# A hybrid diffusion step on one core: the even layer's two attentions in one loop, its projection tail, its output in two halves, and the order at the head and in the odd layer

## The chip, the cores and the metric

The kernel runs on one NeuronCore of a Trainium2 chip. TensorE (PE) multiplies, VectorE (DVE) and ScalarE (ACT) work on vectors and read PSUM, GpSimd (POOL) does elementwise work in SBUF, SyncE (SP) issues the transfers. The metric is the device time of one execution in microseconds, the median of the runs.

## The reference

One inference step of a trunk of two layers for 128 context tokens and 512 latent tokens (640 in all), with a model width of 1024. Each layer is a half-step SwiGLU FFN (hidden width 2816), a mixer, and another half-step FFN, each with an RMSNorm whose scale, shift and gate come from a conditioning vector. The final RMSNorm gives the outputs.

The mixer of the even layer is what the change is mostly about:

```python
cq, ckv, krope, qd, kd, vd = jnp.split(h @ w_in, EVEN_CUTS, axis=-1)
q = (rmsnorm(cq, q_norm) @ w_uq).reshape(b, t, H_A, NOPE_A + ROPE_A)      # 8 heads of 64 + 32
kv = (ckv @ w_ukv).reshape(b, tk, H_A, NOPE_A + V_A)
o_a = mla_attend(q_nope, q_rope, kv[..., :NOPE_A], krope, kv[..., NOPE_A:])
o_b = diff_attend(q1, q2, k1, k2, vd, lam)          # softmax(s1) - lam * softmax(s2), 4 heads of 2 x 64
o_b = rmsnorm(o_b, subln) * (1.0 - lam_init)
return jnp.concatenate([o_a, o_b], axis=-1) @ w_out
```

Latent tokens get a rotary turn of q and k and read 128 cached tokens and all 640 of their step less the context's own (640 keys); context tokens read only the 128 context tokens and get no rotary turn. The odd layer's mixer has two bidirectional gated recurrences, worked in chunks of 128 tokens. Outputs beside the two token arrays are the new caches and states of the context tokens.

## The kernel before

**Layout and arithmetic.** Activations lie with features on partitions: `x` is 8 tiles of 128 features x 640 tokens. A product of the projections and FFNs is exact to fp32 through three products of split numbers: `hh`/`hl` are the high and low part of the normed input, `wh`/`wl` those of a weight unit, and `part_products` does high x high, high x low and low x high, each in two pieces of the token axis (384 and 256, with two more columns that carry the shift of the norm, so 386). Lines 2502, 2504 and 2506 of the profile are these three. A weight unit (1 MB) is loaded by SP to `raw`, copied to `wh` by ACT (`split`, line 2157), and `wl = raw - wh` is made by POOL (`split_lo`, line 2117). There are two slots. `unit_tile` is 8 contraction tiles x 3 products x 2 pieces.

**The norm.** `norm_sum` (lines 2537, 2538) sums the squares over partitions on PE, ACT makes `rstd` (lines 2162 to 2164, Ln then Exp), and the tiles of the next product are scaled by `rstd` only when DVE takes them out of PSUM (`scaled_out`, line 335). So the product can start before `rstd` is known, but PSUM is freed only after. ACT's `z_high` (line 2177) and DVE's `z_low` (line 2346) make `hh` and `hl`.

**Order.** Each engine has one queue, written out by hand, and counts on semaphores hold them together. The phases are ffn0, even, ffn1, ffn2, odd, ffn3.

**The head.** x is turned on PE; `mshift` and then `mscale` (4 MB each) are loaded; PE multiplies them with `cs` (line 2629, 16 matmuls of 2 x 512 for each); ACT copies the two rows out (line 2263), PE turns them to columns, DVE adds the bias (line 2471), then `z_consts`, `z_high` and `z_low`, and the first tile of ffn0.

**The even layer.** `even_pe` runs nine units (7 in `EVEN_T`, two value units in `EVEN_TOK`), two tiles each, and after the first unit it does `norm_sum` and waits for `rstd`. With units 5 to 8 it multiplies the q and k tiles by a rotation matrix (`rotate`, line 875), and DVE forms the rotary turn in three operations (`roped`, lines 711 to 713). After the last unit come: turning five value tiles (line 861), the rotation of the shared rotary key, turning the caches and the context's outputs, the queries head by head (8 products of 96 rows, each with its own rotation of 96 x 512), values of the latent attention (lines 954 to 956), and the keys of head 0 (lines 972 to 974).

Then 40 steps of latent attention (8 heads x 5 blocks of 128 queries), and only then 20 steps of differential attention. For one step: scores on PE into one of two PSUM buffers (`scores_a`, lines 987 to 990; `scores_d`, lines 1045 to 1048, two score arrays for one step), the row maximum on DVE (line 789), the exponential on ACT (line 629), the scaling on DVE (line 819; for a differential step 839, 840 and 842), the transposes of the probabilities on PE (`turn_p`, line 861), their copies on ACT (636, 637), the product with the values on PE (`weigh`, line 1018) and its copy by DVE (804, 806). After each differential head comes `diff_norm` (lines 678 to 684 on ACT, 1056 and 1057 on PE, 811 on DVE); for heads 0 to 2 PE waits in its queue for ACT's result. The last head's norm stands ahead of the output product. `out_pe` takes four units of 256 output columns with all 8 contraction tiles.

**The odd layer.** Its output product already runs in two halves of four contraction tiles (`out_tile`), among the last steps of the recurrence. POOL makes the low parts of the first half (line 1213) in its queue between two weight units. DVE forms `qret` (line 1684) between the second and the third state update.

Of the kernel before, what the change touches and what calls it, by code (L numbers as in the profile page):

```python
# [66 lines left out]
EVEN_T = (0, 256, 512, 672, 928, 1184, 1440)  # L67
EVEN_TOK = (1696, 1952)
# [5 lines left out]
EVEN_UNITS = len(EVEN_T) + len(EVEN_TOK) + 3 + OUT_UNITS  # L74
# [45 lines left out]
def build(nc, a, phases=PHASES):  # L120
# [79 lines left out]
    mrow, _ = view("mrow", [2, 2 * D], at_a + 4 * (TOK // P + DT) * D, end_a)  # L200
# [12 lines left out]
    head_in = [sem("shift_in"), sem("scale_in")]  # L213
    head_mm, mrow_ok = sem("head_mm"), sem("mrow_ok")
# [46 lines left out]
    for name in phases:  # L261
# [5 lines left out]
        else:  # L267

            res_base[name] = n_res
            n_res += 8 if name == "odd" else 4  # L270
# [29 lines left out]

    proj_mm = [sem("proj_mm0"), sem("proj_mm1")]
# [6 lines left out]
    proj_n = {"even": (0, 0, 0), "odd": ((len(EVEN_T) + len(EVEN_TOK), 5, DT) if "even" in phases else (0, 0, 0))}  # L308
# [4 lines left out]

    def turned_unit_pe(pe, unit_tile, n0, done, r):

        pe.wait_ge(w_lo, n0 + 1)
        for m in range(2):
            pe.wait_ge(res_ok[m], res_before[phases[r]])
            if done:
                pe.wait_ge(scaled[m], done)  # L320
            unit_tile(n0 % 2, m, DT, wide(hh), wide(hl), wide_of((psG, psU)[m], 0), True, True,
                      (lambda k: input_split(pe, r, k)) if m == 0 else None).then_inc(proj_mm[m], 1)
# [22 lines left out]
    def turned_values(pe, turn, src, first, done):  # L345

        for j in range(TOK // P):
            if done + j >= 2:
                pe.wait_ge(v_turned[(done + j) % 2], (done + j) // 2)
            ps = (psG, psU)[(done + j) % 2][:, 2, :]  # L350
            for k in range(4):
                ins = turn(ps[:, k * P:(k + 1) * P], src[:, first + k, j * P:(j + 1) * P])
            ins.then_inc(v_turn, 1)

    def values_out(eng, copy, side, dst, done):

        for j in range(TOK // P):
            if (done + j) % 2 == side:
                eng.wait_ge(v_turn, done + j + 1)
                copy(dst(j), (psG, psU)[side][:, 2, :]).then_inc(v_turned[side], 1)  # L360

# [18 lines left out]
    def out_act(act, split, res_squares, z_high, z_shift_high, name, base):  # L380
        r = norm_of[name] + 1
        last = name == phases[-1]

        def pair(i, s, more):
            o = i * 2 + s
            z_high(r, o, 0, res_base[name] + 1)
            if more:
# [2348 lines left out]
```

## Time and profile before

| | before |
|---|---|
| median of 3 runs | 2878.29 us (2877.61 to 2880.95) |
| the profiled execution's own time | 2879.18 us |
| its span | 2877.9 us |
| PE busy | 2739.2 us, 95% of the span |
| DVE, ACT, POOL busy | 1614.4, 921.8, 1030.1 us |
| mean granted TensorE clock | 0.974 |
| HBM traffic | 89 GB/s over the span |

The span is the time from the first to the last instruction. Engines overlap, so their busy times do not add up. A granted clock of 1.0 is 2.4 GHz, 0.5 is 1.2 GHz, and what stands between them is a mean over a stretch with both. Matmuls are pipelined, so the busy time of PE counts a matmul at half the clock as twice as long.

### The profile page before, as it was taken

The page shows a single profiled execution, that of the slowest core. Times are in us where ns is not written, and L with a number is a line of the kernel's source. Part 1 is how long each engine was busy: PE and PEld are TensorE (multiplying, and loading weights), DVE is VectorE, ACT ScalarE, POOL GpSimd, SP SyncE. Part 2 cuts the span into 40 slices and gives each one's busy share as a digit, 9 for nine tenths or more (in the row PEclk, how much of TensorE's full clock was granted, in tenths as well). Part 3 has the DMA queues.
Part 4 walks back from the last instruction along what each step waited for, and adds up shares of the span by engine and source line. Part 5 has one row for each costly group of instructions (what it writes and reads, how often), then busy time and mean ns, then how long its engine had stood idle before and what let it go on. Part 6 is the DMA issues. An engine that isn't in the chain of part 4 may idle for free.

```text
span 2877.9 us, 45113 instructions
## 1 busy us (share of the span) xinstructions
PE 2739.2 (95%) x17963; PEld 2612.1 (91%) x17963; DVE 1614.4 (56%) x2410; ACT 921.8 (32%) x1236; POOL 1030.1 (36%) x300
## 2 busy tenths in 40 slices
PE   6999999998798799999999999999999899999997
PEld 3999999997576599999999999999998799999997
DVE  4888598426556558943885898214474653111124
ACT  3322122442245543321224331123432544321222
POOL 1434344433101024443444344435431313444442
PEclk9999999999898799999999999999999999999999
DMA  6443442321100023423423443221321112222211
GB/s 245 132 142 114 137 147 79 110 74 45 40 1 16 1 73 122 141 81 124 146 90 130 146 132 117 74 81 55 107 59 52 57 40 73 73 66 81 72 60 64
DMA packets 210124, 258.90 MB, mean 90 GB/s; under 512 B 4964, under 2 KB 170472, under 8 KB 210024
## 3 DMA queue, kind: packets, MB, share of 16 engines
q1 hardware_dynamic: 209352, 254.88, 26.9%
q10 hardware_dynamic: 672, 2.62, 0.2%
q8 instruction: 71, 1.16, 0.2%
q14 instruction: 29, 0.24, 0.0%
HBM read 253.66 MB, written 3.82 MB: 89 GB/s over the span
## 4 chain that ended last, share of the span: by engine, by line
PE 86%; DVE 5%; issue 5%; POOL 2%; ACT 2%; DMA 1%; SPq 0%; DVEq 0%; ACTq 0%; POOLq 0%
PE psU L2506 12%; PE psU L2502 12%; PE psU L2504 12%; PE psG L2502 12%; PE psG L2506 12%; PE psG L2504 12%; PE psB L1018 2%; POOL wl L2117 2%; PE psG L861 1%; ACT pr L629 1%; PE psG L987 1%; PE psU L987 1%; DMA mshift<-in_mod_w 1%; PE psG L1045 1%; PE psG L2629 0%
## 5 line engine op out<-in xcount | busy, mean ns | idle before, releaser
L2117 POOL TENSOR_TENSOR wl<-raw,wh 128x2048 fp32r<-128x2048 f32 x185 | 867.7, 4691 | 1219.9 <-ACT wh L2157 1219.9
L2157 ACT CAST wh<-raw 128x2048 fp32r<-128x2048 f32 x185 | 353.3, 1910 | 717.4 <-PE psU L2506 440.9
L2301 DVE SCALAR_TENSOR_TENSOR macc<-mraw,cs,macc 128x512 f32<-128x512 f32 x448 | 488.0, 1157 | 0.0
L2502 PE MATMUL psG<-hh,wh 128*128 128x386 f32 x1744 | 407.7, 315 | 21.2 <-DVE hl L2346 16.8
L2502 PE MATMUL psU<-hh,wh 128*128 128x386 f32 x1760 | 404.2, 311 | 1.5 <-issue 1.5
L2506 PE MATMUL psU<-hh,wl 128*128 128x386 f32 x1760 | 404.7, 311 | 0.0
L2504 PE MATMUL psU<-hl,wh 128*128 128x386 f32 x1760 | 404.1, 311 | 0.0
L2506 PE MATMUL psG<-hh,wl 128*128 128x386 f32 x1744 | 402.8, 312 | 0.0
L2504 PE MATMUL psG<-hl,wh 128*128 128x386 f32 x1744 | 401.9, 312 | 0.0
L2128 POOL TENSOR_TENSOR al<-af,ah 128x640 f32 x88 | 131.6, 1496 | 467.8 <-ACT ah L2214 467.8
L2502 PEld LDWEIGHTS psG<-hh,wh 128*128 128x128 f32 x1744 | 271.4, 191 | 25.8 <-POOL wl L2117 11.1
L2502 PEld LDWEIGHTS psU<-hh,wh 128*128 128x128 f32 x1760 | 271.3, 190 | 3.0 <-issue 2.7
L2504 PEld LDWEIGHTS psU<-hl,wh 128*128 128x128 f32 x1760 | 270.9, 189 | 0.0
L2504 PEld LDWEIGHTS psG<-hl,wh 128*128 128x128 f32 x1744 | 270.2, 190 | 0.0
L2506 PEld LDWEIGHTS psU<-hh,wl 128*128 128x128 f32 x1760 | 270.2, 189 | 0.0
L2506 PEld LDWEIGHTS psG<-hh,wl 128*128 128x128 f32 x1744 | 269.1, 190 | 0.0
L2214 ACT CAST ah<-af 128x640 f32 (+1 forms) x88 | 63.8, 725 | 531.3 <-DVE af L2425 531.3
L2418 DVE TENSOR_TENSOR af<-psU,rstd 128x386 f32<-128x386 f32 (+1 forms) x176 | 74.3, 485 | 268.8 <-PE psU L2506 268.8
L2410 DVE TENSOR_TENSOR sg<-psG,rstd 128x386 f32<-128x386 f32 (+1 forms) x176 | 74.1, 483 | 194.6 <-PE psG L2506 194.6
L2361 DVE SCALAR_TENSOR_TENSOR x<-psG,hgate,x 128x384 f32 (+1 forms) x132 | 49.9, 434 | 230.9 <-PE psG L2506 230.9
L2502 PE MATMUL psG<-ah,wh 128*128 128x384 f32 x704 | 162.3, 312 | 10.1 <-POOL wl L2117 10.1
L2504 PE MATMUL psG<-al,wh 128*128 128x384 f32 x704 | 160.9, 310 | 0.0
(552 smaller groups left out, 4056.4 us busy)
## 6 DMA issues: line engine op xcount, KB each, us to landing
mraw<-in_mod_w SPq DMA_DIRECT2D x64, 1024.0 KB, 5.0
raw<-in_ffn_w_gate SPq DMA_DIRECT2D x44, 1024.0 KB, 5.3
raw<-in_ffn_w_up SPq DMA_DIRECT2D x44, 1024.0 KB, 5.2
raw<-in_ffn_w_down SPq DMA_DIRECT2D x32, 768.0 KB, 4.3
raw<-in_ffn_w_down SPq DMA_DIRECT2D x32, 640.0 KB, 4.0
raw<-in_odd_w_in SPq DMA_DIRECT2D x12, 1024.0 KB, 5.2
raw<-in_even_w_in SPq DMA_DIRECT2D x9, 1024.0 KB, 5.1
mshift<-in_mod_w SPq DMA_DIRECT2D x1, 4096.0 KB, 14.6
```

What stands on the lines that cost most here:

```text
L987: nc.tensor.matmul(buffers(s)[:, 0:512], q, kt[:, h % 2, 0:512], start=True, stop=True)
L1018: ins = nc.tensor.matmul(out, v, pt[:, n % 2, k], start=k == 0, stop=k == kn - 1)
L2117: nc.gpsimd.tensor_tensor(wl[:, slot], raw[:, slot], wh[:, slot].bitcast(F32), ALU.subtract).then_inc(w_lo, 1)
L2128: nc.gpsimd.tensor_tensor(tile_of(al, i * 2 + m), af[:, m, SH:WID], tile_of(ah, i * 2 + m).bitcast(F32), ALU.subtract).then_inc(a_lo, 1)
L2157: nc.scalar.copy(wh[:, slot], raw[:, slot]).then_inc(w_hi, 1)
L2214: nc.scalar.copy(tile_of(ah, i * 2 + m), af[:, m, SH:WID]).then_inc(a_hi, 1)
L2301: ins = nc.vector.scalar_tensor_tensor(out=macc[:, c], in0=mraw[:, s, k], scalar=scalar, in1=macc[:, c], op0=ALU.mult, op1=ALU.add)
L2410: ins = nc.vector.tensor_tensor(sg[:, m, a0:a1], ps, rstd[:, a0:a1], ALU.mult)
L2418: ins = nc.vector.tensor_tensor(af[:, m, a0:a1], ps, rstd[:, a0:a1], ALU.mult)
L2502: nc.tensor.matmul(ps, lhs_h, rhs_h[:, lo:hi], start=first, stop=False)
L2504: nc.tensor.matmul(ps, lhs_h, rhs_l[:, lo:hi], start=False, stop=False)
L2506: ins = nc.tensor.matmul(ps, lhs_l, rhs_h[:, lo:hi], start=False, stop=last)
```

## The change

1. The projection of the even layer has its units in another order: the two value units come fourth and fifth. The turns of the values, the rotation of the shared key and six of the eight head rotations stand between projection tiles. `norm_sum` stands after the first tile, and PE no longer waits for `rstd` there.
2. The queries are six products of 128 rows in place of eight of 96: for four heads two products of the position-free parts (two heads each) and one of the four rotary parts. `query_parts` reorders the columns when ACT and POOL split the weights, so that two rotations of 128 x 512 serve all heads. The splits of both query units stand in the projection. ACT takes over the copies of the turned caches and outputs.
3. The attention steps run in one sequence `SEQ`: one differential step, two latent steps, 18 times, then four latent and two differential steps. Score arrays are counted in units, and `AHEAD` says how far their matmuls run ahead.
4. The differential norm is done once for all heads after the last step, in five matmuls of 512 columns.
5. The output product runs in two halves of four contraction tiles, the first with the latent heads. Two of its tiles stand in the last steps of the attention. Each output tile gets its residual addition twice.
6. At the head the scale is loaded and worked first, the shift after the first weight unit. Each of the two products is four column groups of 256 output columns (partitions 0, 32, 64, 96), and ACT and DVE share the copies. `z_high` and `z_low` run before the shift is there.
7. In the odd layer DVE makes the low parts in place of POOL, and `qret` stands after the last state update.

The core of the diff:

```diff
+EVEN_PROJ = ((0, 0), (256, 2), (512, 4), (1696, 14), (1952, 16), (672, 6), (928, 8), (1184, 10), (1440, 12))
...
+    HEAD_BANKS = (psA, psB, psG[:, 2, :], psU[:, 2, :])
+    def head_rows(eng, copy, side, b):
+        eng.wait_ge(head_mm, b + 1)
+        for g in (side, side + 2):
+            ins = copy(mrow[32 * g:32 * g + 2, b], (psG, psU)[b][32 * g:32 * g + 2, 0, 0:2 * P])
+        ins.then_inc(mrow_ok[side], 1)
...
+    SEQ = []
+    for _i in range(18):
+        SEQ += [D_STEPS[_i], A_STEPS[2 * _i], A_STEPS[2 * _i + 1]]
+    SEQ += A_STEPS[36:] + D_STEPS[18:]
...
+    AHEAD = [min(UNIT_OF[n + 1] + 2, N_SCORES) for n in range(NS)]
...
+        # PE
+        def head_rotated(c):
+            u = 5 + c // 2
+            pe.wait_ge(proj_ok[c % 2], u + 1)
+            rotate(1 + c, 1, P, proj[:, ROPED[c], 0:T_LAT])
+        def queries(i):
+            n = EB + EU + i // 3
+            pe.wait_ge(w_lo, n + 1)
+            ps = (psG, psU)[i % 2]
+            for k in range(3):
+                pe.wait_ge(e_lo, k + 1)
+                w = slice(k * 384 + i % 3 * P, k * 384 + (i % 3 + 1) * P)
+                ins = part_products(wh[:, n % 2, w], wl[:, n % 2, w], cqh[:, k], cql[:, k], runs_alone(ps), k == 0, k == 2)
+            ins.then_inc(e_q, 1)
+        tile(0, 0)
+        norm_sum(r, mods_at["even"])
+        tile(0, 1)
...
+        tile(5, 0)
+        for m in range(2):
+            pe.wait_ge(proj_ok[m], 5)
+        values(0)
+        values(1)
+        tile(5, 1)
+        pe.wait_ge(e_rt, 2)
+        rotate(0, 0, ROPE_A, proj[0:ROPE_A, KR, 0:T_LAT])
+        values(2)
+        values(3)
+        tile(6, 0)
+        values(4)
...
+        for n in range(NS):
+            if next_keys(n) is not None:
+                head_keys(next_keys(n), n)
+            for u in range(AHEAD[n - 1] if n else UNIT_OF[1], AHEAD[n]):
+                scores(u)
+            if n == NS - 1:
+                weigh(n - 1)
+                pe.wait_ge(e_ex, N_SCORES)
+                out_tile(0, 0)
+                turn_p(n)
+            else:
+                turn_p(n)
+                if n:
+                    weigh(n - 1)
+        out_tile(0, 1)
+        weigh(NS - 1)
+        out_tile(0, 2)
+        out_tile(0, 3)
+        pe.wait_ge(d_sq, 4)
+        pe.wait_ge(e_o, NS)
+        means(psA[:, :], n_sqd[:, :, T_LAT:TOK])
...
+        # DVE, one step of the loop
+            for v in range(u, UNIT_OF[n + 1]):
+                inverse(v)
+            if kind == "A":
+                nc.vector.tensor_scalar(p1, p1, stat[:, 3, u % 4:u % 4 + 1], None, ALU.mult).then_inc(e_p, 1)
+            else:
...
+            if n >= 2:
+                heads_out(n - 2)
+            if next_keys(n) is not None:
+                keys_out(next_keys(n))
+            for v in range(AHEAD[n - 1] if n else UNIT_OF[1], AHEAD[n]):
+                maximum(v)
...
     def odd_pool(pool, st, split_lo):
-        for k in range(H_C):
-            pool.wait_ge(o_hi, o0 + k + 1)
-            nc.gpsimd.tensor_tensor(odd_l(k), feat[:, GR + k], odd_h(k).bitcast(F32), ALU.subtract).then_inc(o_lo, 1)
...
+        # odd layer, DVE, ahead of scaled(11, 0)
+        for k in range(H_C):
+            dve.wait_ge(o_hi, o0 + k + 1)
+            nc.vector.tensor_tensor(odd_l(k), feat[:, GR + k], odd_h(k).bitcast(F32), ALU.subtract).then_inc(o_lo, 1)
...
-        for b, w in enumerate((mshift, mscale)):
+        for b, w in enumerate((mscale, mshift)):
             pe.wait_ge(head_in[b], 16)
-            for half in range(2):
-                for k in range(DT):
-                    ins = nc.tensor.matmul((psG, psU)[b][0:2, half, :], cs[:, k], w[:, k, half * 512:(half + 1) * 512],
+            for k in range(DT):
+                for g in range(4):
+                    ins = nc.tensor.matmul((psG, psU)[b][32 * g:32 * g + 2, 0, 0:2 * P], cs[:, k], w[:, k, g * 2 * P:(g + 1) * 2 * P],
                                            start=k == 0, stop=k == DT - 1)
```

## Rows read from the trace of the kernel before

**Rows 1.** Stretches: us; PE, PEld, DVE, ACT, POOL busy; PE clock; DMA share; GB/s.
```profile
694.60:713.80 19.20, 8.84 (x38) 5.75 (x37) 15.13 (x21) 4.84 (x10) 8.20 (x3) 0.67 0.00 1
...
774.70:892.00 117.30, 116.12 (x708) 84.82 (x709) 70.41 (x202) 57.53 (x156) 0.00 (x0) 1.00 0.00 1
892.00:1017.40 125.40, 95.16 (x436) 67.88 (x434) 75.14 (x209) 64.31 (x146) 15.15 (x7) 0.74 0.03 9
```

**Rows 2.** Timeline of the head: start, us, engine, line, operation, idle before.
```profile
20.40 13.89 PE L2629 MATMUL psG<-mshift,cs 128*2 128x512 f32 x32 [2.73 <-DMA mshift<-in_mod_w]
...
34.13 13.90 PE L2629 MATMUL psU<-mscale,cs 128*2 128x512 f32 x32
...
55.41 11.80 DVE L2346 SCALAR_TENSOR_TENSOR hl<-x,g,hh 128x512 fp32r<-128x512 f32 x16
...
60.83 0.87 PE L2502 MATMUL psG<-hh,wh 128*128 128x386 f32 x2 [11.06 <-DVE hl L2346]
```

**Rows 3.** DMA issues: transfer, count, KB, us from issue to landing.
```profile
mshift<-in_mod_w SPq DMA_DIRECT2D x1, 4096.0 KB, 14.6
mscale<-in_mod_w SPq DMA_DIRECT2D x1, 4096.0 KB, 24.3
```

**Rows 4.** Timeline of PE, products into column halves, odd layer.
```profile
2273.94 1.04 PE L1793 MATMUL psB<-rv,kst_r 128*64 128x128 f32 x16
```

**Rows 5.** The chain that ended last, at the norm of the even layer.
```profile
563.46 0.65 PE psA L2537 x2
...
568.93 0.87 PE psG L2502 x2
...
574.62 0.45 PE psG L2504 x2
```

**Rows 6.** Timeline of PE: projection, then the tail up to the first scores.
```profile
692.86 1.02 PE L875 MATMUL psA<-proj,rot 128*128 128x512 f32 x2
...
703.26 1.11 PE L861 MATMUL psU<-ident,vt_e 128*128 128x128 f32 x4 [5.29 <-DVE vd L360]
...
735.53 0.82 PE L2502 MATMUL psU<-cqh,wh 128*96 128x384 f32 x2 [6.25 <-issue]
...
774.71 1.10 PE L987 MATMUL psG<-kt,qa 96*128 96x512 f32 x2 [0.73 <-DVE kt L781]
```

**Rows 7.** Timeline of DVE and POOL, same tail.
```profile
695.43 4.88 DVE L713 TENSOR_TENSOR proj<-proj,rope_e 128x512 f32<-128x512 f32 x1
...
701.79 0.69 DVE L713 TENSOR_TENSOR proj<-proj,rope_e 128x512 f32<-128x512 f32 x1
...
695.03 4.72 POOL L2117 TENSOR_TENSOR wl<-raw,wh 128x2048 fp32r<-128x2048 f32 x1 [11.13 <-ACT wh L2157]
```

**Rows 8.** Timeline of the attention, all engines.
```profile
802.57 1.13 PE L987 MATMUL psG<-kt,qa 96*128 96x512 f32 x2
...
804.40 1.31 PE L1018 MATMUL psB<-pt,va 128*64 128x128 f32 x10
805.63 1.13 PE L987 MATMUL psU<-kt,qa 96*128 96x512 f32 x2
...
931.14 0.89 DVE L842 SCALAR_TENSOR_TENSOR pr<-pr,stat,pr 128x640 f32<-128x640 f32 x1
...
932.14 0.81 DVE L789 TENSOR_REDUCE stat<-psG 128x1 f32<-128x640 f32 x1
...
933.24 0.79 ACT L629 ACTIVATE pr<-psG,stat 128x640 f32<-128x640 f32 x1 [2.41 <-DVE stat L790]
```

**Rows 9.** Waits of PE between 893 and 1018 us: total, times, longest.
```profile
PE psB L1018 <- ACT af L684: 9.3, 3, 3.1
PE psG L861 <- DVE pr L842: 8.7, 8, 1.7
```

**Rows 10.** Timeline of PE at the ends of the odd layer's output.
```profile
2298.29 0.79 PE L1830 MATMUL psU<-am,rv 128*128 128x128 f32 x2 [7.75 <-DVE am L1533]
...
2387.87 0.57 PE L2502 MATMUL psG<-hh,wh 128*128 128x386 f32 x2 [1.89 <-DVE hl L2346]
```

More of the change, by code:

```diff
@@ new lines, in even_act @@
+        log_of(3, n_sqd[:, 1, 0:T_LAT], bank_g)
+        log_of(4, n_sqd[:, 2, 0:T_LAT], bank_u)
+        log_of(5, n_sqd[:, 3, 0:T_LAT], psA[:, :])
+        act.wait_ge(d_ln, 5)
+        for h in range(H_B):
+            nc.scalar.activation(n_sqd[:, h], n_sqd[:, h], ACT.Exp, scale=-0.5).then_inc(d_rt, 1)
+        act.wait_ge(down_mm[1], rb + 2)
+        split(EB + EU + 5)
+        for k in range(4, 8):
+            act.wait_ge(o_ok, o0 + k + 1)
+            copy(even_h(k), proj[:, QD + k - 4]).then_inc(o_hi, 1)
@@ L686, in even_dve @@
+        act.wait_ge(down_mm[1], rb + 4)
+        split(EB + EU + 6)
+        act.wait_ge(stored, 16 * 4)
+        z_shift_high(r)
+        more = phases[-1] != "even"
+        for o in range(4):
+            z_high(r, o, 0, rb + 5)
+            if more and o % 2:
+                act.wait_ge(down_mm[1], rb + 4 + o + 1)
+                split(EB + EU + 7 + o // 2)
+            z_high(r, o, 1, rb + 5)
+            for m in range(2):
+                res_squares(r, o, m, rb + 5)
     def even_dve(dve, st, residual, add_squares, gate_of, z_low, z_consts):
@@ new lines, in even_pe @@
+        values(3)
+        tile(6, 0)
+        values(4)
+        tile(6, 1)
+        head_rotated(0)
+        head_rotated(1)
+        tile(7, 0)
+        tile(7, 1)
+        head_rotated(2)
+        head_rotated(3)
+        tile(8, 0)
+        head_rotated(4)
+        head_rotated(5)
+        tile(8, 1)
+        pe.wait_ge(scaled[0], EU)
+        queries(0)
+        pe.wait_ge(scaled[1], EU)
+        queries(1)
+        head_rotated(6)
+        head_rotated(7)
+        for side in range(2):
+            pe.wait_ge(e_qo[side], 1)
@@ new lines, in means @@
+        def means(bank, src):
+            nc.tensor.matmul(bank, ones[:], src, start=True, stop=True).then_inc(d_mm, 1)
+        pe.wait_ge(c_out, 4)
+        for side in range(2):
+            pe.wait_ge(e_qo[side], 4)
+        pe.wait_ge(e_qr, 2)
+        pe.wait_ge(e_roped, 9)
+        for u in range(UNIT_OF[1]):
+            scores(u)
+        pe.wait_ge(e_roped, 11)
+        pe.wait_ge(e_qc, 2)
+        pe.wait_ge(e_kr, 1)
+        head_keys(0, 0)
+        for side in range(2):
+            pe.wait_ge(e_vo[side], 3)
@@ L1074, in build @@
+        for t in range(8):
+            out_tile(1, t)
     OB = unit_base.get("odd", 0)
```

978 lines of the change are left out of this document (493 added, 485 removed).

## The prediction

> **What bounds the kernel now.** The page first: TensorE is busy for 2739.2 of 2877.9 us. The four FFN phases are filled, so a gain can only come from stretches in which PE stands still, runs at half clock, or does work that goes away. The table of stretches shows three kinds in the even layer [rows 1]. Between 694.6 and 713.8 us PE is busy for 8.8 of 19.2 us at a mean clock of 0.67. The latent attention (774.7 to 892.0) keeps PE at 116.1 of 117.3 us with the clock at 1.00: PE is its bound. The differential attention (892.0 to 1017.4) has PE at 95.2 of 125.4 us with the clock at 0.74, while DVE has 75.1 and ACT 64.3: no engine is full, and a chain from engine to engine sets the pace. The timeline of the head shows PE's two products of 13.9 us each and the first tile of ffn0 at 60.83 [rows 2]. The chain that ended last has a hole at the even layer's norm [rows 5].
>
> **The head.** PE's start of ffn0 is the end of one chain: shift loaded at 20.3, two products, rows out, `hh`, `hl`. In the new order the scale is the first 4 MB and lands at 20.3 as the shift did [rows 3]. Its product has the same 8192 output columns, in four groups of partitions. Lower bound of the time: four at once, 13.9 / 4 = 3.5 us; upper bound: one after the other, 13.9. The nearest rows: eight products of 128 columns that alternate between two column halves (16 records) take 1.04 us, 0.13 each [rows 4]; five of the same width in one half (10 records) take 1.31, 0.26 each [rows 8]. Two halves do run at once; I take four, 3.5 us, so 24. ACT splits the first weight unit first, then rows, turns and bias take the 4.6 us that lie between the last product (48.0) and `hh` now, so `hh` begins near 28.5. `hl` takes 11.8 us for 16 operations with one POOL split over it [rows 2], so 40.5. The shift comes third in the queue: the second 4 MB landed at 6.2 + 24.3 = 30.5 [rows 3], and one unit of 1 MB lies between, so 33.5; 3.5 of product, then the same 4.6 us, slowed by ACT's second split: 43 to 44. PE starts 16 us earlier (8 if the groups run in turn: 34.3 + 13.9 + 4 = 52).
>
> A page of the Trainium skill weighs against the four at once: "TensorE: Matmul & The Clock Gate", Part 3, gives three column tiles a measured 2.38 times, not 3. By it, as an estimate, the product takes 13.9 / 3.2 = 4.4 us and the head gives 15. No row here has four groups.
>
> **The norm.** PE waits from 564.5 to 568.93 and runs at half clock until 575.07: 4.4 us and half of 5.7, so 7 us [rows 5]. After the change the sum comes one tile (7.1 us) earlier, and the second tile hides the 3 us of ACT. What is late next is DVE's reading of the first tile, 4 us before PE wants that bank. Gain 7.
>
> **Moved into the projection.** Five value tiles of four turns (1.11 us at half clock, so 0.55 at full) and one rotation (two take 1.02 us and more, records overlapping; 0.86 each between their starts) [rows 6] stand in PE's queue between tiles: +3.7 with their gaps, all on the path. DVE's and ACT's copies lie beside tiles of 7.1 us.
>
> **The tail up to the first scores.** Now 692.86 to 774.71, 81.9 us [rows 6]. Its holes: 5.3 us at the values, 6.3 at the second query unit's split, others before rotations, each with a stretch at half clock behind it. What is left after the change, at full clock: six query products of 3 x 3 x 0.295 = 2.65 us (15.9; eight now), two head and two query rotations (3.4; ten now), 14 turns of caches and outputs (3.0), 36 value products of 0.23 (8.3): 31 us. I add 3 for the handshakes between query products and ACT's or DVE's copies: 34. Gain 48. What hides the splits: both query units are split while PE works tiles 8 and 9, the unit for the values while PE does three query products and 14 turns (13 us against 1.9 + 4.7). If the cover goes, the queue of DVE is the cause: it has 8.4 us of query rotation behind a POOL split. Bounds of the gain: 38 (one lock of 4.7 us at each of two places) and 51.
>
> **The attention loop.** PE's work: the latent part stays at 116. A full latent step takes 805.63 - 802.57 = 3.06 us [rows 8]. A differential step is one score array more, 1.07: 4.13; 16 of these and four short ones of 1.0 make 70. Together 186 us against 242.7 now. Can ACT and DVE follow? For one group of a differential and two latent steps (18 of them) PE has 4.13 + 2 x 3.06 + 0.8 (share of the keys) = 11.0 us. DVE: four maxima of 0.93, two latent scalings with copies (0.95), the differential scaling (two reciprocals, 0.55, 0.19, 0.89 and a copy: 2.4), keys 0.5: 8.5 us. ACT: four exponentials of 0.9, three pairs of copies of 0.75, 0.5: 6.4 us. So PE remains the largest. In order of time: the exponentials of the differential step end at 0; its scaling ends at 1.9; the next two maxima end at 3.1 and 4.1; ACT's next exponential ends at 4.05, when PE ends the turns and products it has (3.9) and takes the next score array; the group closes at 10.2. It is nearly without slack on DVE, so I charge 1 us of wait to each group, 18 us, from nothing (the latent part loses 1.2 us in 117 now) up to 2 us a group. First latency +3, two output tiles that now lie in the last steps +7, last step +1: 215. Gain 28 (10 to 44). The norm waits of 9.3 us and the 8.7 us for the scaling [rows 9] are within what goes. PE's clock, 0.74 now, must be near 1.00 for this.
>
> **The output.** Before: 1017.4 to the norm sum of ffn1 at 1085.8, 68.4 us. After: 14 of 16 tiles of 3.55 (49.7), five means of 0.86 (4.3), the first FFN tile 7.1, and waits: 1.5 for the first residuals, 1.5 for ACT's split and POOL behind the norm, 3 at the end, as the odd layer's same form has 1.89 for the last `hl` [rows 10]. That is 67: gain 1 (-4 to +3). The second addition to x costs DVE 8 x 1.1 us beside PE.
>
> **The odd layer.** PE waits 7.75 us for DVE [rows 10]. DVE loses some 4 us less to POOL's low parts and takes 3.3 us for four of its own; `qret` only changes its place ahead of the same reading of tile 11. Gain 2 (-1 to 5).
>
> **Sum.** 16 + 7 - 3.7 + 48 + 28 + 1 + 2 = 98 us. The profiled execution took 2879.2, so 2781; the median of the runs shown is 0.9 lower: 2780.
>
> **Rivals.** (a) DVE becomes the bound of the loop. It has 8.5 of 11.0 us, and it serves in order: a maximum stands behind a scaling that waits for ACT (ACT's 2.41 us of idle before an exponential is that wait [rows 8]). At 13 us a group: +36, 2816. Against it: the hand schedule closes at 10.2. (b) POOL holds DVE. An addition of two SBUF tiles took 4.88 us beside a split of 4.72, and 0.69 without [rows 7]. In the loop lie two splits and four low parts of about 1.6 us, 16 us of POOL, and in the tail two splits. If all of it lands on the path: +16 to +20, 2799. The Trainium skill states it as a lock ("SBUF — State Buffer", Who interferes with whom): the later of the two blocks wholly, and copies in some modes too. The trace agrees for two inputs. (c) The column groups run in turn: +8, 2788. (d) The other side: the loop does not overlap. Each step then waits for its own chain (scores 1.08, maximum 0.97, exponential 0.9, scaling 0.7, turns 0.75, copy 0.75, product 1.23: 6.4 us, 7.9 for a differential one), 20.7 us a group, +170 us: 2950. It decides from 16.5 us a group on. For it: the differential part does take 6.3 us a step. Against it: the latent part, with the same two buffers, takes 3.06.
>
> **Chances.** The forecast (2765 to 2792) 0.55; (a) 0.14; (b) 0.12; (c) 0.06, inside the likeliest range's edge; better than forecast (loop or tail at the upper ends) 0.07; (d) or another large new wait 0.06, two thirds of it slower than before. The range is 2762 to 2812. Faster by over 0.2% (5.8 us, what a measurement here can tell from no change): 0.94; within: 0.02; slower: 0.04.
>
> **What would show it.** PE's first tile of ffn0 near 44 us, and the first product (scale) ending near 24. No wait for `rstd` behind the first even tile. From the last projection tile to the first scores 34 us. In the loop, PE over 90% busy, clock 1.00, 11 to 12 us for a group, and about 215 us from the first scores to the last value product. Wrong if PE's waits for DVE's scaling in the loop exceed 30 us, if the clock stays under 0.9 there, or if the tail exceeds 45 us.

## The result, and the profile after

The changed kernel took 2808.53 us (median of 4 executions, 2803.39 to 2813.54), the kernel before 2877.95 beside it: ratio 0.9755, interval 0.9739 to 0.9771. Forecast were 2780 and a range of 2762 to 2812. So 69 us were gained where 98 were forecast: the direction and the range hold, the point does not, and the sum behind it is wrong in two places, the attention loop above all.

The profiled execution took 2813.54 us against 2879.18, 65.6 less. Cut at the same events of PE in both traces (its first tile of ffn0; the first even tile behind the wait for `hl`; the end of the last projection tile, which for the kernel before is the rotation at 692.86; the first scores; the end of the last value product; the norm sums of the next phases), the two stand so. For the kernel before, the attention is counted to 1017.4, as in the prediction: that is the sum of the last differential norm, 1.15 us behind the end of its last value product at 1016.25. "Again" is a second trace of the changed kernel, from an execution of 2806.17 us.

| stretch | before | after | again | forecast gain | gain in the profiled pair |
|---|---|---|---|---|---|
| head, up to PE's first tile of ffn0 | 60.83 | 45.58 | 45.16 | 16 | 15.3 |
| ffn0, to the first even tile | 494.4 | 497.7 | 497.1 | 0 | -3.3 |
| projection, with the norm and what moved in | 137.7 | 134.3 | 134.4 | 7 - 3.7 | 3.3 |
| tail, to the first scores | 81.9 | 34.4 | 31.8 | 48 | 47.4 |
| attention, first scores to last value product | 242.7 | 233.5 | 233.4 | 28 | 9.2 |
| output, to the norm sum of ffn1 | 68.4 | 74.7 | 70.7 | 1 | -6.3 |
| ffn1 and ffn2 | 967.8 | 968.0 | 966.4 | 0 | -0.2 |
| odd layer | 336.0 | 334.6 | 336.5 | 2 | 1.3 |
| ffn3, to the end of the span | 488.4 | 489.3 | 489.5 | 0 | -1.0 |

The views of the profile after, in the order of the steps. First the head, a timeline (start, us, engine, line, operation, idle before and what ended it), which answers to [rows 2]:

```profile
21.23 5.21 PE L2768 MATMUL psG<-mscale,cs 128*2 128x256 f32 x64 [3.72 <-DMA mscale<-in_mod_w]
...
27.13 4.50 POOL L2232 TENSOR_TENSOR wl<-raw,wh 128x2048 fp32r<-128x2048 f32 x1 [25.15 <-ACT wh L2272]
28.50 3.16 DVE L2604 SCALAR_TENSOR_TENSOR g<-mod,vec 128x16 f32<-128x16 f32 x1
...
34.64 5.33 PE L2768 MATMUL psU<-mshift,cs 128*2 128x256 f32 x64 [6.61 <-DMA mshift<-in_mod_w]
...
40.91 4.50 POOL L2232 TENSOR_TENSOR wl<-raw,wh 128x2048 fp32r<-128x2048 f32 x1 [9.28 <-ACT wh L2272]
...
42.78 2.66 DVE L2613 TENSOR_TENSOR hl<-mod,hh 128x16 fp32r<-128x16 f32 x1 [0.40 <-ACT hh L2303]
```

The product of 13.9 us takes 5.21 in four column groups. But the mean clock was 0.69 in these 5.21 us and 1.00 in the 13.89 of the kernel before. Three later traces of the same product ("order taken back", "paired, other order around" and "head wait") have the clock at 1.00 there, and it takes 3.63 us; this is "head wait":

```profile
21.09 3.63 PE L2769 MATMUL psG<-mscale,cs 128*2 128x256 f32 x64 [2.31 <-DMA mscale<-in_mod_w]
```

Two DVE operations of 16 columns last 3.16 and 2.66 us (the second takes 0.18 in "head wait"): each ends when POOL's operation beside it does (27.13 + 4.50, 40.91 + 4.50).

Then three stretches of the even layer (us; PE, PEld, DVE, ACT, POOL busy; PE clock; DMA share; GB/s): the tail, the attention, the output. The second answers to the last two of [rows 1].

```profile
677.60:712.00 34.40, 31.35 (x168) 26.45 (x166) 17.21 (x30) 19.16 (x41) 14.99 (x6) 0.95 0.32 103
712.00:945.50 233.50, 215.74 (x1189) 155.22 (x1188) 148.64 (x412) 104.58 (x284) 10.69 (x5) 0.95 0.02 7
945.50:1020.20 74.70, 65.08 (x396) 61.26 (x395) 52.80 (x86) 33.64 (x46) 19.20 (x4) 0.95 0.22 75
```

The tail's 47.4 us can be read from such lines. Before, PE stood for 26.1 of 81.9 us at a mean clock of 0.79; now it stands for 3.1 of 34.4 at 0.95. So 23 us are holes that are gone, 15.5 are time at the lower clock (0.21 x 81.9 less 0.05 x 34.4), and 9 are work that went away or moved. No run takes the tail's parts back one by one, so what each of them is worth was not shown.

In the attention PE is at 92% busy and its clock at 0.95 instead of 0.87 over the two parts. Yet it is only 9 us shorter. This is what PE works at a differential step there, from the timeline:

```profile
743.60 1.12 PE L1102 MATMUL psG<-proj 64*128 64x512 f32 x2
744.56 0.38 PE L1102 MATMUL psG<-kdc,proj 64*128 64x128 f32 x2
744.87 0.33 PE L928 MATMUL psG<-ident,pr 128*128 128x128 f32 x1
745.04 1.28 PE L1129 MATMUL psB<-pt,vd 128*128 128x128 f32 x10
746.25 1.12 PE L1102 MATMUL psU<-proj 64*128 64x512 f32 x2
747.21 0.38 PE L1102 MATMUL psU<-kdc,proj 64*128 64x128 f32 x2
```

Each of the two score arrays of a differential step takes 1.27 us (743.60 to 744.87, 746.25 to 747.52), with a value product between them. Last, PE's waits (who for whom: total, times, longest), first in the attention (714 to 945 us), then in the output (945.4 to 1020.2):

```profile
PE psG L1102 <- ACT pr L663: 6.3, 7, 1.2
...
PE psG L928 <- DVE pr L886: 4.4, 8, 1.4
...
PE psG L928 <- DVE pr L881: 3.6, 4, 2.7
```

```profile
PE psG L2641 <- DVE ml_b L908: 5.6, 2, 3.6
PE psG L2641 <- DVE hl L2462: 1.9, 1, 1.9
PE psG L2641 <- DVE x L2477: 1.6, 1, 1.6
```

### The profile page after: what moved, and what is told of

Same layout as the page of the kernel before. It is cut to its first block, busy times and chain, and to the rows that moved or that the text cites. A ratio compares the mean times of both kernels' runs of the same rounds, so it can differ in the third digit from the quotient of the medians.

```text
span 2812.2 us, 44951 instructions
## 1 busy us (share of the span) xinstructions
PE 2705.7 (96%) x17973; PEld 2597.5 (92%) x17973; DVE 1598.1 (57%) x2432; ACT 914.6 (33%) x1252; POOL 1010.4 (36%) x294
## 4 chain that ended last, share of the span: by engine, by line
PE 85%; DVE 6%; issue 4%; ACT 2%; POOL 2%; DMA 0%; SPq 0%; DVEq 0%; ACTq 0%; POOLq 0%
PE psU L2645 13%; PE psU L2641 13%; PE psU L2643 13%; PE psG L2641 12%; PE psG L2645 12%; PE psG L2643 12%; PE psB L1129 2%; POOL wl L2232 1%; PE psG L1102 1%; PE psU L1102 1%; PE psG L928 1%; DVE stat L853 1%; DVE rstd L2487 1%; ACT wh L2272 0%; PE psB L2636 0%
## 5 line engine op out<-in xcount | busy, mean ns | idle before, releaser
L2232 POOL TENSOR_TENSOR wl<-raw,wh 128x2048 fp32r<-128x2048 f32 x183 | 858.2, 4690 | 1077.7 <-ACT wh L2272 1077.7
L2477 DVE SCALAR_TENSOR_TENSOR x<-psG,hgate,x 128x384 f32 (+1 forms) x144 | 54.3, 432 | 241.2 <-PE psG L2645 241.2
L2641 PE MATMUL psG<-ah,wh 128*128 128x384 f32 x704 | 162.9, 313 | 10.2 <-POOL wl L2232 10.2
L2645 PE MATMUL psG<-ah,wl 128*128 128x384 f32 x704 | 161.5, 311 | 0.0
```

What stands on the lines that cost most here:

```text
L2232: nc.gpsimd.tensor_tensor(wl[:, slot], raw[:, slot], wh[:, slot].bitcast(F32), ALU.subtract).then_inc(w_lo, 1)
L2641: nc.tensor.matmul(ps, lhs_h, rhs_h[:, lo:hi], start=first, stop=False)
L2645: ins = nc.tensor.matmul(ps, lhs_l, rhs_h[:, lo:hi], start=False, stop=last)
```

## The experiments

All are edits of the changed kernel unless the text says otherwise. Ratios are to the kernel before, on the same chip; one kernel's executions scatter by up to 15 us here, so a difference of a few microseconds is read from the stretches and not from the total. Attention and output are these stretches in microseconds, each from one trace (233.5 and 74.7 in the first trace of the change, 242.7 and 68.4 before).

| kernel | median us | ratio, interval | attention | output |
|---|---|---|---|---|
| again | 2807.62 | 0.9753 (0.9739, 0.9766) | 233.4 | 70.7 |
| order taken back | 2806.13 | 0.9746 (0.9731, 0.9761) | 231.0 | 70.7 |
| scores paired | 2809.85 | 0.9754 (0.9741, 0.9768) | 234.2 | 74.6 |
| paired, other order around | 2814.97 | 0.9775 (0.9762, 0.9788) | 236.4 | 70.7 |
| before, without the four norms | 2854.43 | 0.9910 (0.9895, 0.9925) | 221.0 | - |
| short maximum | 2791.22 | 0.9685 (0.9671, 0.9700) | 216.4 | 70.8 |
| short maximum, paired | 2790.53 | 0.9684 (0.9669, 0.9699) | 219.6 | 74.8 |
| low parts on DVE | 2806.68 | 0.9740 (0.9727, 0.9753) | 230.3 | 74.8 |
| output split early | 2796.99 | 0.9714 (0.9701, 0.9728) | 231.6 | 66.9 |
| head wait | 2803.87 | 0.9739 (0.9725, 0.9752) | 228.5 | 74.6 |
| head wait and output split | 2800.00 | 0.9719 (0.9706, 0.9732) | 228.4 | 66.9 |
| all three small ones | 2802.71 | 0.9720 (0.9704, 0.9735) | 231.4 | 67.0 |

**Again.** The changed kernel, not edited.

> The changed kernel once more, unchanged. Its four executions lay between 2803.4 and 2813.5 us, so the same is expected: 2803 to 2814, with a second trace that tells which of the numbers of the first are steady. Theory 1 (the stretch of ffn0, 497.7 us from PE's first tile to the first even tile against 494.4 before, holds a steady new wait of 3.5 us for POOL's low part at 273): the wait and the 497.7 come again. Rival (it is a chance meeting of DVE and POOL): the stretch falls back to about 494.5, and the execution is near 2804 to 2806.

Theory 1 came out: in each further trace of the changed head PE waits 3.2 to 3.6 us for POOL's low part near 273 us, 2.1 before. So 1 to 3 us of the head are given back in ffn0. What makes that unit late was not traced further. The attention came out at 233.4 again; the tail and the output differ by 2.6 and 4.0 between two traces of one kernel, through waits and what the clock does behind them.

**Order taken back.**

```diff
-    for _i in range(18):
-        SEQ += [D_STEPS[_i], A_STEPS[2 * _i], A_STEPS[2 * _i + 1]]
-    SEQ += A_STEPS[36:] + D_STEPS[18:]
+    SEQ += D_STEPS[:18] + A_STEPS + D_STEPS[18:]
```

> The order of the steps alone is taken back: 18 differential steps, then all 40 latent ones, then the last two differential ones; all else is as in the change. Theory (the interleaving itself brought the gain of the loop): the differential part runs at its chain again, about 6.3 us a step and half clock for much of it, the latent part at 3.1 us a step; 18 x 6.0 + 40 x 2.95 + the last two steps and two output tiles (about 18) = 244 to 252 from the first scores to the last value product, against 233: kernel 2819 to 2827. Rival (the interleaving brought nothing, the gain came from elsewhere in the stretch): within 3 us of the change.

The rival came out: 231.0 us against 233.4 and 233.5. The edit does one thing more than its name says. Where differential steps follow each other, the look-ahead takes in both score arrays of a step, and PE works them side by side, or overlapped in part (766.48 and 767.35):

```profile
782.06 0.69 PE L1100 MATMUL psG<-proj 64*128 64x512 f32 x1
782.07 0.69 PE L1100 MATMUL psU<-proj 64*128 64x512 f32 x1
```

In the change they stand apart, and PE's busy time in the stretch is 215.7 us against 207.4 here. The kernel that interleaves and has them together is "scores paired" below, and it takes 234.2. So with either look-ahead, interleaving the two attentions, which names the change, gains nothing here. The stretches of this kernel, the 18 differential steps and then nearly all latent ones:

```profile
710.60:799.00 88.40, 71.02 (x372) 50.77 (x372) 66.77 (x186) 38.80 (x104) 0.00 (x0) 0.88 0.03 10
799.00:912.00 113.00, 111.76 (x681) 81.13 (x679) 69.07 (x191) 58.13 (x154) 8.10 (x4) 1.00 0.00 1
```

A differential step by itself takes 4.9 us (88.4 / 18), not the 6.3 (125.4 / 20) of the kernel before [rows 1]. Something else was in those 125.4 us.

**The kernel before, without the four norms of the differential heads.**

```diff
-            if i in (8, 13, 18):
-                diff_norm_act(act, st, (i - 8) // 5)
...
-            if i in (8, 13, 18):
-                diff_norm_sum((i - 8) // 5)
-                pe.wait_ge(d_rt, (i - 8) // 5 + 1)
...
-            nc.vector.scalar_tensor_tensor(out=proj[:, QD + h], in0=proj[:, QD + h], scalar=vec[:, g:g + 1], in1=af[:, 1, 0:TOK],
-                                           op0=ALU.mult, op1=ALU.mult).then_inc(o_ok, 1)
+            nc.vector.tensor_copy(lam[:, 3:4], lam[:, 1:2]).then_inc(o_ok, 1)
```

> The kernel before the change, with the norms of the four differential heads left out: no squares, sums, logarithms, exponentials and products for them, and no waits for them (the output is then not the reference's). Theory 2, formed from the order that was taken back: it was these norms, ten us of standing engines each, and not the chain of a differential step, that made the differential part long before. Without them a full step takes 4.8 us as in the order taken back: 16 x 4.8 + 4 x 3.1 = 89 instead of 125.4, so the two attentions take 206 to 212 instead of 242.7, and the kernel 2842 to 2850 (some further microseconds at the last norm). Rival, the reading of the prediction (each differential step is held by its own chain at 6.3 us, the norms add only their 9.3 us of waits): the loop stays at 231 to 235 and the kernel at 2866 to 2871.

221.0 us: 21.7 less than before (20.5 up to the same event, the end of the last value product), between the two expectations (12 above theory 2's middle, 12 below the rival's). From one head to the next, PE's value products lie 30.8 us apart in the kernel before (948.24 to 979.07) and 24.3 here (961.54 to 985.79). So a norm costs 6.6 us in the loop, more than twice the wait that it is booked with in [rows 9]. Theory 2 was wrong to count a short step at 3.1: the 24.3 us are 4.9 a step with the short one in it. The holes can be seen in the kernel before, two stretches of 10 us:

```profile
940.00:950.00 10.00, 5.10 (x21) 3.55 (x21) 3.63 (x14) 7.50 (x16) 0.00 (x0) 0.67 0.00 0
...
970.00:980.00 10.00, 4.84 (x20) 3.07 (x19) 3.48 (x14) 7.87 (x18) 0.00 (x0) 0.71 0.01 2
```

PE and DVE are at about half or less and ACT at 75% and more: square, logarithm and exponential stand in ACT's queue ahead of the exponentials of the next step. The timeline of the kernel before has this norm from its square to PE's next value product:

```profile
941.16 0.76 ACT L678 ACTIVATE af<-proj 128x640 f32<-128x640 f32 x1
941.93 1.28 ACT L682 ACT_TABLE_LOAD   x1
...
946.15 1.28 ACT L684 ACT_TABLE_LOAD   x1
947.45 0.74 ACT L684 ACTIVATE af<-af 128x640 f32<-128x640 f32 x1
...
948.24 2.50 PE L1018 MATMUL psB<-pt,vd 128*128 128x128 f32 x10 [3.09 <-ACT af L684]
```

ACT is in the norm for 7.0 us, and 2.6 of them are two loads of its function table, one ahead of the logarithm and one ahead of the exponential. The kernel before has eight such loads for its four norms, the change two (946.63 and 962.92).

The change takes the norms out of the loop and makes them in the output, all at once. The two output tiles of some 4 us that now lie in the stretch leave 221.0 + 8 = 229, and the changed kernels measured 228 to 234. So the norms that left are enough for the loop's whole gain.

**Scores paired.** The look-ahead of PE and DVE never ends between the two score arrays of a differential step.

```diff
     AHEAD = [min(UNIT_OF[n + 1] + 2, N_SCORES) for n in range(NS)]
+    AHEAD = [v - 1 if v - 1 in [UNIT_OF[d] for d in range(NS) if SEQ[d][0] == "D"] else v for v in AHEAD]
```

> The two score arrays of a differential step are issued next to each other again (the look-ahead never stops between them). Theory 1: side by side, in partitions 0 to 63 and 64 to 127, the two take about 1.3 us together (in the kernel before, 936.05 to 937.60 for both), apart 1.27 each; 16 full steps give PE 16 x 1.2 = 19 us less work in the loop (213 us busy now, about 195 then). The look-ahead loses one step, so part comes back as waits: by DVE's and ACT's chain (two maxima, two exponentials, the scaling of 2 us) a group closes at about 10.7 us instead of the 11.7 measured, so the loop goes from 233 to 215 to 225 and the kernel is 8 to 18 us faster than the change: 2790 to 2800. Rival A (the look-ahead is worth more than the pairing): PE's waits grow by more than 19 us, the loop stays at 233 or above, kernel 2805 to 2825. Rival B (they do not overlap even when adjacent): PE's busy time stays at 213 and nothing is won.

Its timeline at such a step, and its stretch:

```profile
779.08 0.81 PE L1103 MATMUL psG<-proj 64*128 64x512 f32 x1
779.10 0.81 PE L1103 MATMUL psU<-proj 64*128 64x512 f32 x1
779.73 0.59 PE L1103 MATMUL psG<-proj 64*128 64x512 f32 x1
779.74 0.59 PE L1103 MATMUL psU<-proj 64*128 64x512 f32 x1
```

```profile
712.40:946.50 234.10, 198.75 (x1189) 144.00 (x1188) 150.48 (x412) 105.30 (x284) 10.66 (x5) 0.96 0.02 6
```

The two arrays, 64 partitions each, do run at once: PE's busy time falls by 17.0 us (215.7 to 198.8). Its work without what the lower clock stretches is 189 us (198.8 less 0.04 x 234.1), less than the 194 that the prediction counted. Rival A came out all the same: the time comes back as waits, PE's for DVE's scaling go from 8.0 to 23.4 us:

```profile
PE psG L929 <- DVE pr L882: 17.1, 11, 2.7
PE psG L929 <- DVE pr L887: 6.3, 15, 1.4
```

**Paired, with another order around it.** The diff shows PE's and ACT's part; DVE takes `heads_out(n - 2)` ahead of its scaling.

```diff
+            elif n and "D" in (SEQ[n][0], SEQ[n - 1][0]):
+                weigh(n - 1)
+                turn_p(n)
...
+            if n >= 1 and SEQ[n - 1][0] == "D":
+                turned(n - 1)
             for u in range(UNIT_OF[n], UNIT_OF[n + 1]):
                 exponentials(u)
```

> The pairing of the differential scores together with another order around it: at a differential step and the one behind it PE takes the value product of the step before ahead of the turns, ACT copies the turned differential step out ahead of the next exponential, and DVE takes heads out ahead of the scaling. Theory 1 (with the scores paired PE has 198 us of work in 233, and stands for DVE's scaling, 23 us, because the value product that could fill that time is queued behind the turns): the waits for the scaling fall from 23 to 8 to 14 us, the loop from 234 to 219 to 226, the kernel 8 to 15 us under the paired one: 2795 to 2802. Rival (the chain of DVE and ACT of 11.7 us a group is full whatever PE does): the loop stays within 3 us of 234, the waits only change their names.

The rival came out, 236.4 us. The waits for the scaling fell as forecast (23.4 to 9.9 us), and new ones took their place: 8.4 us for ACT's copy of the turned step, 8.6 for DVE's copies out of psB.

**Short maximum, paired and unpaired.** A row maximum over a fifth of the columns gives the same softmax as long as nothing overflows, which nothing excludes for other inputs.

```diff
-            st.link(nc.vector.tensor_reduce(stat[:, 0, u % 4:u % 4 + 1], buffers(u)[:, 0:n_keys(j)], AX.X, ALU.max))
+            st.link(nc.vector.tensor_reduce(stat[:, 0, u % 4:u % 4 + 1], buffers(u)[:, 0:P], AX.X, ALU.max))
```

> The same short maximum in the kernel of the change, with its scores unpaired. Theory 3 (there PE's own work, 205 us without the two output tiles' 8, is the bound, and of DVE only the 17 us of waits and the half clock behind them are to be had): the loop 233 -> 217 to 225, so less than with the paired scores, and PE's clock 0.98 to 1.00 in it; kernel 2790 to 2800. Rival (DVE's chain is the bound here too): the loop gives as much as in the paired kernel, to 214 or below.

> The differential scores paired, and DVE takes the row maximum over the first 128 of the 640 columns only (0.29 us instead of 0.82; softmax is the same with any shift that does not overflow). Theory 3 (with the scores paired the loop is held by DVE's serial chain of maxima, exponentials and scaling, 11.8 us a group, and PE, 198 us busy of 233, waits): four maxima a group become 0.53 us shorter each, 2.1 us, two to four of them on the chain: 18 groups x 1.1 to 2.1 = 20 to 38 us, bounded by PE's own work of 186 to 198 us: the loop 234 -> 200 to 214, kernel 2775 to 2790. Rival (DVE is not what the chain waits for; ACT or the two score buffers set 11.8 us): the loop stays above 228, kernel above 2802.

The attention of the unpaired and of the paired kernel:

```profile
712.30:928.80 216.50, 207.77 (x1189) 149.96 (x1188) 116.40 (x412) 104.92 (x284) 10.69 (x5) 0.98 0.02 7
```

```profile
711.40:930.90 219.50, 197.03 (x1189) 145.50 (x1188) 117.22 (x412) 103.67 (x284) 10.67 (x5) 0.95 0.02 6
```

Both kernels gain 16 to 17 us in total (2791.2 and 2790.5), the best of the study. (Against "again"; the ratios say some 20.) With 32 us less on DVE the unpaired loop falls by 17, just past its expectation, and PE is busy for 96% at a clock of 0.98: here PE is the bound. In the paired one theory 3 is half right: 219.5, 5 above its range and well under the rival's 228, with 22.5 us of PE idle still. So DVE's maxima are on the chain in both; why the paired loop does not go below PE's new work stays open. It is not DVE's total, which is 117 of 219.5 us.

**Output split early.**

```diff
+        act.wait_ge(down_mm[1], rb + 2)
+        split(EB + EU + 5)
         log_of(5, n_sqd[:, 3, 0:T_LAT], psA[:, :])
...
-        act.wait_ge(down_mm[1], rb + 2)
-        split(EB + EU + 5)
         for k in range(4, 8):
```

> ACT splits the third weight unit of the output ahead of the fifth logarithm, in the 3.7 us in which it waits for the fifth mean, instead of behind the exponentials. Theory 1: POOL's low part (5.0 us) then lies at about 960 to 965, ahead of DVE's four norm products (7.6 us beside it, 4.5 without), so PE's 5.6 us of waits for the low parts of the mixed values and 2 to 4 us of half clock behind them go or shrink: stretch of the output 74.7 -> 67 to 70, kernel 5 to 8 us faster than the change. Rival (PE waits there for the chain of means, logarithms and exponentials, POOL's part is hidden anyway): the wait stays above 4 us, nothing is won or up to 2 us lost.

Theory 1 came out: the stretch takes 66.9 us, the clock is 1.00 in it, and PE's wait for `ml_b` is gone, 1.3 us more of waits for the residuals against it. DVE's four norm products and four low parts in the change and then in this kernel:

```profile
966.79 7.59 DVE L903 SCALAR_TENSOR_TENSOR proj<-proj,vec,n_sqd 128x640 f32<-128x640 f32 x4
...
968.72 4.98 POOL L2232 TENSOR_TENSOR wl<-raw,wh 128x2048 fp32r<-128x2048 f32 x1 [31.81 <-ACT wh L2272]
...
975.35 7.35 DVE L908 TENSOR_TENSOR ml_b<-proj,mh_b 128x640 fp32r<-128x640 f32 x4
```

```profile
961.89 3.26 DVE L903 SCALAR_TENSOR_TENSOR proj<-proj,vec,n_sqd 128x640 f32<-128x640 f32 x4
966.12 3.02 DVE L908 TENSOR_TENSOR ml_b<-proj,mh_b 128x640 fp32r<-128x640 f32 x4
```

The same instructions take 3.26 and 3.02 us without a POOL operation beside them. The total fell by 10.6 us against "again", more than the 4 to 8 of the stretch; the rest is scatter elsewhere in the traces.

**Head wait.** POOL waits for the shift's low part.

```diff
+        pool.wait_ge(sh_lo, 1)
         split_lo(1, 1)
```

> POOL makes the low part of the second weight unit of ffn0 only when the low part of the shift is there. Theory 1 (the small operation on the shift took 2.66 us instead of 0.2 because POOL's part of 4.5 us had begun at 40.91, and PE's first tile waited for it): PE starts ffn0 at 42.7 to 43.3 instead of 45.2 to 46.9, kernel 2 to 3 us faster: 2804 to 2806. Rival (the second unit's low part, which now starts 2 to 3 us later, is itself late for PE's second tile, or the chain through the shift's product gives no more): start at 43, but a new wait of 1 us or more at the second tile, nothing won.

The operation on the shift takes 0.18 us instead of 2.66, and PE's first tile is at 44.37; the two later kernels with this edit have it at 43.29 and 43.46. Here the shift's copies out of PSUM came 1.7 us later than in "again". No new wait came at the second tile; POOL's part now holds another DVE operation (5.20 us instead of 0.87), which PE does not wait for there. Theory 1 is right in kind, with 1 to 2 us at PE's first tile; the total's 3.8 us are not clear of the intervals.

**Low parts on DVE.** `head_lo` and the low part of the output's second unit are issued by DVE behind its maxima.

```diff
-        for k in range(3):
-            head_lo(k)
-        split_lo(EB + EU + 4, (EB + EU + 4) % 2)
-        head_lo(3)
...
+            if n in lows:
+                head_lo(lows[n])
+            if n == AT["A", H_A - 1, 0] + 1:
+                u5 = EB + EU + 4
+                dve.wait_ge(w_lo, u5)
+                dve.wait_ge(w_hi, u5 + 1)
+                nc.vector.tensor_tensor(wl[:, u5 % 2], raw[:, u5 % 2], wh[:, u5 % 2].bitcast(F32), ALU.subtract).then_inc(w_lo, 1)
```

> The low parts that POOL makes inside the attention loop (four of 1.54 us for the heads, one of 4.5 us for a weight unit) are made by DVE instead, 0.7 us each and 2.2 us; the rest is the change. Theory 1 (POOL holds DVE: the scaling at 912.39 took 3.69 us instead of 0.55, PE stood 2.7 us and ran at half clock for 8 us behind it): the wait and the slow spell at 913 to 924 go, 5 to 7 us; DVE's own 5 us of new work costs PE 1 to 3: the loop 233.4 -> 228 to 231, kernel 2802 to 2806 beside 2807.6. Rival (DVE's time is what bounds the loop, and 5 us more of it are 5 us more): the loop stays at 233 to 236, kernel 2807 to 2811.

230.3 us is in the theory's range, but loops that were not edited measured 228.5 to 233.5. Undecided.

**The small ones together.**

> The same without the low parts on DVE: only the output's split and the head's wait. If they add by the ratios: 2807.6 - 15 = 2793; by the stretches 6 to 10 us: 2798 to 2801. Beside it the third edit's own worth is read: theory (POOL's part at 912 costs the loop a wait of 2.7 us and a slow spell): the three together are 2 to 5 us faster than these two; rival (chance): within 1.5 us.

> Three of the edits together: the output's third weight unit split ahead of the fifth logarithm, the low part of ffn0's second weight unit after the shift, and the low parts inside the attention loop on DVE; scores and order as in the change. If the three gains add (11, 4 and 4 us by the ratios 0.9714, 0.9739 and 0.9740 against 0.9753): 2807.6 - 19 = 2789, range 2784 to 2795. By the stretches alone (output 4 to 8 us, head 1 to 2, loop 3) it is 10 to 13: 2795 to 2798; then part of the single ratios was chance.

They don't add by the ratios: 2800.0 and 2802.7. By the stretches the first two come to 6 to 10 us (head 1.9, output 3.8 to 7.8), and the median gained 7.6. The low parts on DVE add nothing on top. Both kernels beat the change and the kernel before; of the single edits that keep the computation as it is, the output's early split is the only one whose gain stands clear of the interval of "again".

## Why the prediction came out as it did

**Right, with its size:** the head, the norm with the moved work, and the tail.

In the head the first tile was forecast at 43 to 44 and measured at 45.6; without the second held operation it is at 43.3 to 44.4. The four column groups do run at once: 3.63 us at full clock against 13.89 is 3.8 times as fast, close to the 3.5 us of the sum, and rival (c) is out. What the sum lacked is the clock, 0.69 there in the profiled execution, which made 5.21 of it, and POOL's hold on the small operation. The Trainium skill ("TensorE: Matmul & The Clock Gate", Part 3) gives three column tiles 2.38 of 3, from which the prediction estimated 3.2 times, 4.4 us, for four; these traces have no case of three, and with four they are faster than that estimate.

The norm and the moved work: 3.3 forecast, 3.3 measured. The tail: 34 us forecast, 34.4 and 31.8 measured. Together these are 66.0 us, as much as the whole difference.

**Wrong: the attention loop, 28 forecast, 9.2 measured.** The step that failed is "so PE remains the largest": that PE's work and 1 us of wait a group set the pace, because the group of DVE and ACT "closes at 10.2". In the steady part five groups with the keys of two heads repeat every 54.66 us (PE's value products at 735.25, 789.92, 844.57 and 899.23), 10.9 a group:

```profile
735.25:789.92 54.67, 51.64 (x287) 36.41 (x286) 36.04 (x103) 25.19 (x70) 1.54 (x1) 0.97 0.00 1
```

By the prediction's terms these five are 4 x 4.13 + 1.0 + 2 x 116 / 8 = 46.5 us of work and 5 of waits, 51.5. Measured are 49.9 of work, 1.7 of lower clock and 3.0 of waits. Over 18 groups that makes 11 of the 19 us. Most of the rest lies at the loop's end: from 899.23 to 945.5 PE stands for 6.7 us, at a mean clock of 0.86. Four things are to be said of that step.

*What the 125.4 us held.* The prediction read the differential part as "a chain from engine to engine" of some 6.3 us a step that overlapping would hide. Its own rival (d) repeats that figure. The chain is 4.8 to 4.9 us; the rest is the norms, three of them inside the loop. They were in view as 9.3 us of waits [rows 9], and "within what goes"; they measured 20.5 to 21.7 us. This reading does not enter the 215, but it is why the gain was put down to the overlap. The overlap itself gave nothing: 231.0 with the order taken back against 233.4, and 234.2 with the scores paired. In the order taken back, five differential steps take 23.8 us (774.62 to 798.44) and five latent ones with their keys 15.2 (804.51 to 819.75); 23.8 + 2 x 15.2 is 54.3, against 54.7 interleaved.

*PE's work.* Forecast 186 + 7 + 1 = 194 us. Measured: 215.7 busy, less what the half clock stretches (0.05 x 233.5 = 11.7), 204. Of these 10 us the larger part is the differential step: 1.07 was charged for the second score array, but alone it takes 1.27, as does the first, so with turns of 0.7 a step is 4.5 instead of 4.13. In the kernel before the two ran side by side (936.05 and 936.07 for the first of each), which the look-ahead of the new order ends. No rival had this.

*The waits behind it.* That work is not the whole cause. With the scores paired it is 189 us, under the forecast, and the loop still takes 234.1: five groups repeat every 55.6 to 56.7 us, and PE waits for the scaling. So with PE's work under the forecast a group still takes 11.1 to 11.3 us as a mean, where the order in time closed a full one at 10.2. That DVE's maxima are on that chain is shown by their shortening; which link makes the rest was not found.

*The clock.* 1.00 was forecast and 0.95 granted: 11.7 us, in spells of 3 to 7 us. They begin during a stop of PE or a little behind it: 1.2 us for an exponential up to 773.8, 2.7 for DVE's scaling up to 916.1. The waits themselves are 17.8 us where 21 were forecast. So 204 + 11.7 + 17.8 = 233.5 against 194 + 21 = 215.

The prediction named as its test "wrong if PE's waits for DVE's scaling exceed 30 us or the clock stays under 0.9": they were 8.0 us and 0.95, so this sign did not appear though the term was wrong. It did not cover the case that the work itself was larger.

**Wrong: the output, +1 forecast, -6.3 measured.** The prediction charged "3 at the end" and 1.5 for POOL behind the norm. The four norms, now in one block, meet two POOL parts: 5.6 us of waits for the low parts and 3.7 lost at a clock of 0.95. That is rival (b), the lock, at a place where it was booked at 1.5; in the loop, where it was expected, one wait of 2.7 us can be put down to it (the scaling at 912.39). The Trainium skill states it as a lock between DVE and POOL ("SBUF — State Buffer", Who interferes with whom); the traces agree for additions and products of two SBUF tiles and for the scaling of one SBUF tile (3.69 instead of 0.55 at 912.39, from POOL's 911.22 to 915.73), while a maximum over PSUM at 911.27 took its usual 0.82.

**Rival (a)** (DVE the bound, 13 us a group, 2816) was nearer than its chance of 0.14: DVE's maxima are on the loop's chain, as their shortening by 32 us of DVE's time and 17 of the loop's shows, but a group took 10.9 us and DVE was busy for two thirds of it (36.0 of 54.7 us). **Not in the sum:** 3.3 us in ffn0, of which 1.4 is the longer wait for POOL near 273. **The odd layer:** 1.3 and, in "again", -0.5 for a forecast of 2 (-1 to 5): nothing that can be told from scatter.

That the range held is luck in part: errors of 19 us in the loop, 7 in the output and 3 in ffn0 lay within a bound that was drawn for other causes (rival (b)'s, 2799, and (a)'s, 2816). The likeliest span, 2765 to 2792, was missed.

## What to carry to other kernels

Before an overlap is priced by the average time of a step, cut the stretch by what its steps have in common and what only some have: the mean of 6.3 us held 4.8 us of step and a norm every fifth step, and the cheap cure was to move the norm. Look for table loads in such a norm: gathering four norms turned eight loads into two. Two orders of the same steps cost the same here, so take an order back before you credit it, and check what else that edit changes: a look-ahead counted in single score arrays parted what was a pair, and putting the pair together again took 17 us off PE's busy time and nothing off the loop. Before you divide two times of PE's work, put the clock of both beside them. When a block of DVE work is gathered at one place, look at which POOL operation starts beside it, and start that one a few microseconds earlier.

## What the runs showed of the hardware

Four column groups of 2 output partitions, 256 columns each, ran 3.8 times as fast as one group with 512 at the same clock of 1.00 (3.63 us in three traces against 13.89, for 64 and 32 records); with the clock at 0.69 they took 5.21. Two score arrays with 64 contraction rows each, in different halves of the partitions, ran together in 1.3 to 1.4 us when they were next to each other in PE's queue, and took 1.27 each when other work stood between them. A DVE operation of 16 columns in SBUF waited until POOL's 4.5 us were over; a DVE maximum over PSUM beside another POOL part did not. A change of ACT between logarithm and exponential cost a table load of 1.28 us. After a stop of PE as short as 1.2 us the granted clock was at its lower level for some 3 us soon after in some places (774 to 780: 0.72 mean) and stayed at 1.00 in others (after 1.04 us at 720.7); such spells are the largest difference seen between two traces of one kernel, whose executions scatter by up to 15 us.
